# Mixture of experts on one core: steps of 32 rows in four column groups instead of 64 rows in two

## The reference, cut to what matters

```python
def _moe(h, gates, w1, w3, w2):
    y = jnp.zeros_like(h)
    for e in range(N_EXPERTS):
        a = jax.nn.silu(h @ w1[e]) * (h @ w3[e])
        y = y + gates[..., e:e + 1].astype(h.dtype) * (a @ w2[e])
    return y
```

## Time and profile before

| what | us |
|---|---|
| median of three runs (1363.28 to 1370.95) | 1368.34 |
| the profiled execution's own time | 1366.75 |
| its span, first to last instruction | 1365.2 |

### The profile page before, as it was taken

One profiled execution on the slowest core, in us unless ns is written; L12 is line 12 of the kernel. 1 busy time (PEld: TensorE's weight loads), 2 busy tenths in 40 slices (PEclk: granted clock), 3 DMA queues, 4 the chain that ended last, 5 costly groups with the idle time before them and its releaser, 6 DMA issues.

```text
span 1365.2 us, 14253 instructions
## 1 busy us (share of the span) xinstructions
PE 1096.2 (80%) x4818; PEld 506.8 (37%) x4819; DVE 356.6 (26%) x685; ACT 296.2 (22%) x527; POOL 205.3 (15%) x244
## 2 busy tenths in 40 slices
PE   3899999999839999987777228998973788977880
PEld 0444666344413333333222114555341333333330
DVE  0420239245301111111100395017242111111115
ACT  0111228301202232232221001206110322211220
POOL 1410000123310111110000254000031100100113
PEclk9899999999869999998888659999985988988895
DMA  9992310734754776689998751420972999999952
GB/s 303 393 417 80 123 62 1 273 128 168 288 222 159 269 249 223 229 319 395 401 395 317 268 203 62 150 97 13 387 277 77 323 387 397 370 398 394 374 202 100
DMA packets 73932, 337.71 MB, mean 247 GB/s; under 512 B 8492, under 2 KB 10668, under 8 KB 61604
## 3 DMA queue, kind: packets, MB, share of 16 engines
q1 hardware_dynamic: 56148, 282.02, 54.3%
q0 software_dynamic: 16272, 54.02, 11.6%
q10 hardware_dynamic: 1472, 1.12, 0.3%
HBM read 305.94 MB, written 31.20 MB: 247 GB/s over the span
## 4 chain that ended last, share of the span: by engine, by line
PE 61%; DMA 18%; DVE 8%; issue 5%; POOL 3%; SPq 2%; ACT 1%; POOLq 0%; DVEq 0%; ACTq 0%
PE PS L1466 17%; PE PS L1296 15%; DMA W<-in_moe_w 14%; PE PS L1479 9%; PE PS L1407 6%; PE PS L1460 3%; PE PS L1252 2%; PE PS L1267 2%; PE PS L1362 2%; PE PS L1242 2%; DMA W<-in_w_ada 2%; DMA H<-xg_rows 1%; PE PS L1472 1%; DMA y_rows<-H 1%; PE PS L1374 1%
## 5 line engine op out<-in xcount | busy, mean ns | idle before, releaser
L1466 PE MATMUL PS<-W,XT 128*64 128x512 f32 x1376 | 331.0, 636 | 79.9 <-DMA W<-in_moe_w 71.9
L1296 PE MATMUL PS<-W,XT 128*128 128x512 f32 (+1 forms) x544 | 217.1, 560 | 2.7 <-ACT RB L690 1.8
L1466 PEld LDWEIGHTS PS<-W,XT 128*64 128x64 f32 x1376 | 112.1, 146 | 268.0 <-issue 258.6
L1479 PE MATMUL PS<-W,AT 128*64 128x512 f32 x688 | 157.1, 598 | 2.0 <-DVE AT L1161 2.0
L835 ACT ACT_TABLE_LOAD x43 | 55.2, 1283 | 435.7 <-PE PS L1460 435.7
L1296 PEld LDWEIGHTS PS<-W,XT 128*128 128x128 f32 x544 | 103.8, 192 | 110.9 <-issue 108.5
L1157 DVE COPY EX<-PS 128x512 f32<-128x512 f32 x43 | 29.7, 692 | 418.4 <-PE PS L1466 418.4
L605 POOL DMA_DIRECT2D H<-xg_rows x45 | 23.6, 525 | 413.0 <-PE PS L1460 342.3
L1407 PE MATMUL PS<-W,XT 128*128 128x512 f32 x192 | 83.1, 593 | 0.0
L1460 PE MATMUL PS<-C,H 64*128 64x64 f32 x360 | 49.3, 279 | 37.0 <-DMA H<-xg_rows 37.0
L1164 DVE COPY H<-PS 128x512 f32<-128x512 f32 x43 | 29.7, 691 | 178.7 <-PE PS L1479 167.9
(11 more groups left out here) (169 smaller groups left out, 925.9 us busy)
## 6 DMA issues: line engine op xcount, KB each, us to landing
W<-in_moe_w SPq DMA_DIRECT2D x96, 2048.0 KB, 13.9
W<-in_w_ada SPq DMA_DIRECT2D x24, 2048.0 KB, 13.7
W<-in_w_in SPq DMA_DIRECT2D x8, 2048.0 KB, 17.0
H<-xg_rows POOLq DMA_DIRECT2D x45, 256.0 KB, 5.8
y_rows<-H POOLq DMA_DIRECT2D x86, 128.0 KB, 7.0
xg_rows<-X POOLq DMA_DIRECT2D x1, 8192.0 KB, 35.6
W<-in_w_out SPq DMA_DIRECT2D x4, 2048.0 KB, 10.1
y_rows<-X POOLq DMA_DIRECT2D x1, 4096.0 KB, 49.0
```

Source lines behind the costliest of these rows:

```text
L1296: mm = pe.matmul(ps[:, 0:cw], XT[:, k, P * t:P * t + P], w[:, k, :], start=(k == 0), stop=(k == KD - 1))
L1466: mm = pe.matmul(UP_PS[ROWS * n:ROWS * n + ROWS, :], XGT[:, k, :], moe_up(3 * p + n)[:, k, :], start=(k == 0), stop=(k == KD - 1), tile_po ...
L1479: mm = pe.matmul(DOWN_PS[ROWS * n:ROWS * n + ROWS, :], ATX[:, k, :], moe_down(3 * p + 2)[:, k, 512 * n:512 * n + 512], start=(k == 0), sto ...
```

## The change

- `ROWS` is 32 and `BLOCKS` 52. Steps are of 32 rows.
- `up` computes four column groups of 32 partitions: the two halves (256 columns) of `w1` and of `w3`; `down` computes four quarters of the output, 256 columns each. A step's `up` has 32 matmuls of 256 columns (before 16 of 512), its `down` 16 of 256 (before 8 of 512).
- The rows of a step are loaded by one transfer onto 64 partitions of 2 KB (the two halves of each row apart), turned by four transposes (before eight), and the activations by two (before four). The weights' rows are laid out to match: each partition of a slot gets two runs of 8 KB (before one of 16 KB).
- Rows are loaded into `XRAW`; ScalarE copies them to `XG` (`stage`), which frees `XRAW` for the next load. The copy of the turned rows to `XGT` moves from ScalarE to VectorE.
- A step's result is stored by one transfer from 128 partitions of 1 KB, from one of two buffers `YO[b]`, each with its own semaphore.
- GpSimd's, ScalarE's and VectorE's loops are written anew for this order; two small operations on VectorE count the steps of each parity (`halves`).
- TensorE's walk over j is gone: an expert's second to fifth step are written out, each inside the `If` of the one before, and a loop from j = 5 stands inside the innermost.

```diff
 BIG = 1e30
-ROWS = 64
-BLOCKS = 2 * NEXP
-MOST = 2 * 4
+ROWS = 32
+BLOCKS = 3 * NEXP + 4
...
         U = EX[:, :, :].rearrange("p t (a b c) -> p t a b c", a=2, b=2)
-        XG = H[0:ROWS, 0:D]
-        YO = H[:, 3072:3584]
-        EXU = EX[:, 0, :]
-        GU = EX[:, 3, 0:4 * ROWS].rearrange("p (k s) -> p k s", k=FE // P)
-        XGT = XT[:, 0, :].rearrange("p (k s) -> p k s", k=KD)
-        ATX = AT[:, 0, 0:4 * ROWS].rearrange("p (k s) -> p k s", k=FE // P)
+        XRAW = H[0:2 * ROWS, 0:D // 2]
+        XG = H[0:2 * ROWS, 1024:1024 + D // 2]
+        YO = [H[:, 3072:3328], H[:, 3328:3584]]
+        EXU = EX[:, 0, 0:256]
+        GU = EX[:, 3, 0:4 * ROWS].rearrange("p (k s) -> p k s", k=2)
+        XGT = XT[:, 0, 0:8 * ROWS].rearrange("p (k s) -> p k s", k=4)
...
                 s = 3 * e + n
-                k = KD if n < 2 else FE // P
-                dst = W[:, s, :].rearrange("p (k n) -> p k n", k=k)
+                k = 4 if n < 2 else 2
+                dst = W[:, s, :].rearrange("p (q x) -> p q x", q=2)
                 src = (moe_w1, moe_w3, moe_w2)[n][L, at, :, :]
-                src = src.rearrange("(p k) n -> p k n", p=P) if isinstance(at, int) else \
-                    src.rearrange("o (p k) n -> p (o k) n", p=P)
+                src = src.rearrange("(q p k) n -> p q (k n)", q=2, p=P) if isinstance(at, int) else \
+                    src.rearrange("o (q p k) n -> p (o q) (k n)", q=2, p=P)
                 sp.dma_start(dst, src).then_inc(w_full[s], 16)
...
+                def step_rows(table, n, q):
+                    rows = table[n * ROWS:n * ROWS + ROWS, :] if isinstance(n, int) else table[bass.ds(n * ROWS, ROWS), :]
+                    return rows.rearrange("t (q c) -> q t c", q=q)
+
                 def load_rows(n):
+                    pool.dma_start(XRAW, step_rows(xg_rows, n, 2)).then_inc(rows_in[L], 16)
+
+                def store_rows(n, b):
+                    pool.dma_start(step_rows(y_rows, n, 4), YO[b]).then_inc(y_written[b][L], 16)
...
+                pool.wait_ge(rows_staged[L], 4)
+                load_rows(4)
+                pool.wait_ge(out_copied[L], 3)
+                store_rows(1, 1)
...
-                with pool.Fori(2, most_steps(L)) as n:
-                    with pool.If(total > n):
-                        wait_apart(pool, rows_turned[L], n + 1)
-                        load_rows(n + 1)
-                        wait_apart(pool, out_copied[L], n)
-                        store_rows(n - 2)
-                    with pool.Else():
-                        pool.nop()
+                with pool.Fori(0, most_steps(L) // 2 - 1) as i:
+                    for b in range(2):
+                        n = 2 * i + (2 + b)
+                        with pool.If(total > n):
+                            wait_apart(pool, rows_staged[L], n + 3)
+                            load_rows(n + 3)
+                            wait_apart(pool, out_copied[L], n + 2)
+                            store_rows(n, b)
+                        with pool.Else():
+                            pool.nop()
+                pool.wait_ge(halves_ready, L + 1)
+                evens, odds = steps_by_half(pool, L)
+                wait_apart(pool, y_written[0][L], evens * 16)
+                wait_apart(pool, y_written[1][L], odds * 16)
+                wait_apart(pool, rows_in[L], total * 16 + 48)
+                wait_apart(pool, rows_staged[L], total + 2)
...
-                def rows_out():
-                    nc.scalar.activation(XGT, ROWS_PS.rearrange("p (k s) -> p k s", k=KD), ACT.Copy).then_inc(xgt_ready[L], 1)
+                def stage():
+                    copy(XG, XRAW, rows_staged[L])
                 total = steps_of_layer(act, L)
                 with act.Fori(0, most_steps(L)) as n:
                     with act.If(total > n):
                         act.wait_ge(rows_turned[L], n + 2)
-                        act.wait_ge(up_done[L], n + 1)
-                        rows_out()
+                        wait_apart(act, rows_in[L], n * 16 + 48)
+                        stage()
                         act.wait_ge(act_turned[L], n + 1)
...
+                def rows_out():
+                    dve.tensor_copy(XGT, ROWS_PS[:, 0:8 * ROWS].rearrange("p (k s) -> p k s", k=4)).then_inc(xgt_ready[L], 1)
...
+                with dve.Fori(0, most_steps(L) // 2 - 1) as i:
+                    for b in range(2):
+                        n = 2 * i + (3 + b)
+                        with dve.If(total > n):
+                            dve.wait_ge(up_done[L], n + 1)
+                            copy_up()
+                            dve.wait_ge(rows_turned[L], n + 2)
+                            rows_out()
+                            dve.wait_ge(down_done[L], n)
+                            wait_apart(dve, y_written[b][L], i * 16 + 16)
+                            copy_out(b)
+                            dve.wait_ge(gate_ready[L], n + 1)
+                            product()
+                        with dve.Else():
+                            with dve.If(total > n - 1):
+                                dve.wait_ge(down_done[L], n)
+                                wait_apart(dve, y_written[b][L], i * 16 + 16)
+                                copy_out(b)
+                            with dve.Else():
...
                 def turn_rows():
-                    turned = XG.rearrange("t (d k) -> t k d", k=KD)
-                    for k in range(KD):
-                        mm = pe.transpose(ROWS_PS[:, ROWS * k:ROWS * k + ROWS], turned[:, k, :], IDENT[0:ROWS, 0:ROWS])
+                    turned = XG.rearrange("s (d k) -> s k d", k=4)
+                    for k in range(4):
+                        mm = pe.transpose(ROWS_PS[:, 2 * ROWS * k:2 * ROWS * k + 2 * ROWS], turned[:, k, :],
+                                          IDENT[0:2 * ROWS, 0:2 * ROWS])
                     mm.then_inc(rows_turned[L], 1)
 
                 def up(p):
                     for k in range(KD):
+                        rows = XGT[:, k % 4, ROWS * (k // 4):ROWS * (k // 4) + ROWS]
                         for n in range(2):
-                            mm = pe.matmul(UP_PS[ROWS * n:ROWS * n + ROWS, :], XGT[:, k, :], moe_up(3 * p + n)[:, k, :],
-                                           start=(k == 0), stop=(k == KD - 1), tile_position=(0, ROWS * n))
+                            for a in range(2):
+                                o = ROWS * (2 * n + a)
+                                mm = pe.matmul(UP_PS[o:o + ROWS, 0:256], rows,
+                                               moe_up(3 * p + n)[:, k, 256 * a:256 * a + 256],
+                                               start=(k == 0), stop=(k == KD - 1), tile_position=(0, o))
                     mm.then_inc(up_done[L], 1)
 
                 def turn_act():
-                    for n in range(FE // P):
-                        mm = pe.transpose(TURN_PS[:, P * n:P * n + P],
-                                          EXU.rearrange("t (f k) -> t k f", k=FE // P)[:, n, :], IDENT)
+                    turned = EXU.rearrange("s (f k) -> s k f", k=2)
+                    for k in range(2):
+                        mm = pe.transpose(TURN_PS[:, P * k:P * k + P], turned[:, k, :], IDENT)
                     mm.then_inc(act_turned[L], 1)
 
                 def down(p):
                     for k in range(FE // P):
-                        for n in range(2):
-                            mm = pe.matmul(DOWN_PS[ROWS * n:ROWS * n + ROWS, :], ATX[:, k, :],
-                                           moe_down(3 * p + 2)[:, k, 512 * n:512 * n + 512],
-                                           start=(k == 0), stop=(k == FE // P - 1), tile_position=(0, ROWS * n))
+                        rows = ATX[:, k % 2, ROWS * (k // 2):ROWS * (k // 2) + ROWS]
+                        for q in range(4):
+                            o = ROWS * q
+                            mm = pe.matmul(DOWN_PS[o:o + ROWS, 0:256], rows,
+                                           moe_down(3 * p + 2)[:, k, 256 * q:256 * q + 256],
+                                           start=(k == 0), stop=(k == FE // P - 1), tile_position=(0, o))
                     mm.then_inc(down_done[L], 1)
...
-                    wait_apart(pe, rows_in[L], step * 16 + 32)
+                    wait_apart(pe, rows_staged[L], step + 2)
...
-                    with pe.If(cnt > ROWS):
-                        with pe.Fori(1, 2 * T) as j:
-                            with pe.If(cnt > j * ROWS):
-                                pe.wait_ge(xgt_ready[L], step + j + 1)
-                                up(p)
-                                rest(p, step + j, p, own)
-                            with pe.Else():
-                                pe.nop()
-                        pe.nop()
+                    def again(j):
+                        pe.wait_ge(xgt_ready[L], step + j + 1)
+                        up(p)
+                        rest(p, step + j, p, own)
+
```

(52 more changed lines are left out.)

70 lines of the change are left out of this document (32 added, 38 removed).

## The result

The changed kernel takes 1556.31 us (median of 4 runs, 1553.44 to 1563.37) against 1366.64 us for the kernel before, run beside it: 1.1417 times as long, 95% interval 1.1386 to 1.1449. The profiled execution spans 1557.0 us (1365.2 before). The forecast was 1339: -28 us came out as +190.

A forecast was written before the change was run, and what follows sets the result against it. TensorE was taken to set the pace early in layer 0's expert stage, the weights' DMA later; 1366.75 + 2 (layer 0) - 25 (layer 1) - 5 (stage ends) + 0.5 (counting, tables) = 1339 us, range 1300 to 1388.

The forecast's parts named there:

- TensorE's step: TensorE's work for one step of rows: 12.31 us with 64 rows becomes 6.42 us with 32.
- Rival 3: TensorE's short records are no cheaper than long ones: step 11.3 us, layer 0 +100, about 1470 us; chance 0.04.
- Reading the counts: Each expert's register loads on TensorE's sequencer, no longer hidden under up: 1.7 us an expert.
- Rows' path: Loading and staging a step's rows takes L + 2.8 us, costing 2.5 us an expert in layer 0.
- L: Landing time of a step's row load: taken as 5.3 us, between 3.5 and 8.9.
- Code size: Skips over written-out steps and the pair loop's end fetch instructions: 3 us each, 1.2 exposed per expert, 3 per pair.
- Walk over j: Empty iterations after an expert's last step: some 7 us saved in layer 0, 7 lost by five-step experts; even.
- Ends: From the last down to the gather at a stage's end: 10.9 us becomes 7.2; -4, in layer 1 -1.
- The sum for layer 1: Layer 1's expert stage: refills from 1055, end at 1303 instead of 1328 after up to 13 lost; -25 us.
- Rival 2: The rows' path is the bound: with L = 8.9, layer 0 +30, layer 1 +13, 1405 us; chance 0.18.
- +2: Layer 0's expert stage: 362 us against 360, with the late experts' refills at the DMA engines' pace.
- Rival 1: The written-out code costs nothing (branches of 0.22 us): layer 0 -20, layer 1 -28, 1314 us; chance 0.22.

The follow-up runs named there:

- e4: The changed kernel with a step's rows loaded by two plain transfers of 32 partitions instead of one: 1489.65 us.
- e6: The changed kernel with two plain row loads and, in place of the written-out steps, a loop ending at the loaded step count: 1391.6 us.
- e7: The changed kernel with two plain row loads, the loop by count and a second buffer of raw rows: 1321.25 us.
- e10: The changed kernel with two raw-row buffers and the loop by count, but each load still the change's one transfer: 1367.69 us.
- e13: The changed kernel with two raw-row buffers, two plain loads, two further steps written out and the loop by count from the third on: 1372.97 us.
- e8: The kernel before (steps of 64 rows) with its walk over j replaced by the loop by count: 1360.1 us.
- e3: The changed kernel with only step 0's rows loaded and the walk over j of before in place of the written-out steps: 1430.94 us.
- e12: The changed kernel with two raw-row buffers, two plain loads, the loop by count and each store as four plain transfers: 1309.33 us.

## Why the prediction was wrong

- **TensorE's step** was right: 6.42 forecast, 6.52 measured. The 66 steps too. Rival 3 is out.
- **Reading the counts** (1.7 us an expert): 1.4 in the chain without loads. Right.
- **Rows' path, the term L:** this step failed first. I took 5.3 us for a landing, between 3.5 and 8.9, since the transfer is halved. Landings are 4.8 to 5.6 us without weight traffic and 13 to 16 under it, above my upper bound. In layer 1's stage they average 9.8 us over 27 loads, and 25 steps of 9.8 + 2.8 are 315 of its 333 us. The bytes were halved, but the new form runs them two packets at a time, sixteen one behind the other, where the kernel before had sixteen and more at once. Without weights the last of them ends 4.9 us after the issue; under weights each of the sixteen also waits for a weight packet of 0.35 us: 3.9 us to the first and 16 x 0.55 = 8.8 for the chain are 12.7 of 13.5. The runs with two plain loads (e4, e6) and the two-buffer pair (e7 1321, e10 1368) show that it is the form of the transfer; the chains in the trace show how. The Trainium skill (DMA: Bandwidth & Descriptors, section Queues, rings and completion order) has the rule that a DMA engine goes round its queue rows a packet at a time. The trace agrees as far as it can tell: under weights the 4096-byte packets of a chain start some 0.55 us apart and without them 0.16. I had drawn from it that a half as long weight packet shortens the wait, without asking how many turns the fullest engine has to wait for.
- **Code size:** this step failed second. A missed fetch was put at 3 us, 1.2 exposed at a skip; the branches take 3.3 to 7.6 us, and most skips are followed by an up that runs in part at the lower clock, which I hadn't counted at all: the 18 ups right behind such a skip take 3.7 to 7.8 us, 6.3 on average, instead of 3.66. I had 22 us for layer 0; over both layers the whole is 140 to 148 us where rows don't cover it. My bounds (0.22 and 8.9 us) held the branch. The Trainium skill (Runtime: NRT & Kernel Launch, section Instruction fetch mechanics) was borne out in direction: the longer loop is fetched again, in all passes but one. By its 128 KiB e13's loop, with 112 KB at most, should have stayed; the trace (nine packets each in two of layer 0's later passes) decides against that.
- **Walk over j**, "even" at -7 and +7: it was hidden before (3 us, e8), so the gain was never there, and at 32 rows it is not (e3).
- **Ends:** I expected 7.2 us from the end of down to the gather; 890.14 to 900.37 is 10.2, since the last store lands in 7.2 and not in 5. Before it was 10.9.
- **The sum for layer 1** has a slip: 1055 + 230 + 2 is 1287 and not 1289. It changes nothing here; the stage took 333 us against 254 forecast, and layer 0's 490 against 362.
- **Rival 2** named the mechanism (the rows' path is the bound when weights flow, from L of about 7) and gave 1405 with L = 8.9. The mechanism was right, its size and the code's price on top of it were not, and its chance of 0.18 was too small.

Where both are mended (e12, 1309.33, with a second raw buffer and plain stores as well), the narrow step gains 55 us, and 51 over the kernel before with the loop by count (e8). That isn't my -28 come true: my sum had 22 us of code, 20 of rows and 7 of the walk in layer 0, which this kernel doesn't have. Its layer 0 ends its last down at 728.7 us, 29 before the 757.9 of the kernel before, where I had +2. Rival 1, the code at nothing, is the nearer sum: 1314 with -20 there.

## What to carry to other kernels

When a transfer changes its form, ask over how many DMA engines its large packets are spread, and not only how many bytes it has: on engines shared with a bulk stream, each packet of the longest chain waits its turn. Under full weight traffic sixteen in a row landed in 13 to 16 us, and each of two plain transfers with the same bytes in 7.6 (median). A part of a program that repeats a number of times known only at run time belongs in a loop whose end is the loaded count: written-out copies cost fetches, a walk with tests costs the sequencer, and both show only when the step gets short enough to lay them bare. Two defects that hide behind each other have to be removed together once, or each looks cheap: the code's price read 21 us here with the rows broken and 148 without.

## What the runs showed of the hardware that I had not expected

- A GpSimd transfer of 64 partitions x 2 KB, whose source has the split outer dimension, leaves 224 packets of 8 bytes beside its 32 of 4096, and the 32 run two at a time; as two plain transfers it leaves none of 8 bytes, and up to sixteen of the 32 run at once. Without weight traffic the first lands in 4.8 to 5.6 us and the plain ones in 2.0 to 3.2; where the weights fill the DMA engines the medians are 13.6 and 7.6.
- A taken branch to code that isn't held costs 3.3 to 4.0 us while the DMA engines are all but idle and 5.6 to 7.6 while they carry weights, though its packet of 16 KB itself takes about 1.1 us. The same skip takes 0.21 us in a pass in which no code is fetched (e13).
- A loop of TensorE instructions that came in four packets of 16 KB was fetched once a layer; one that came in seven was fetched again in about every second pass.
- Right behind such pauses TensorE's next up took 6.3 us on average instead of 3.6, in part at the lower level of the granted clock (0.69 in the one shown): a pause costs more than its length.
